# A decoder trunk on one core: two pieces of VectorE's work given to GpSimd

## The reference

```python
def s5_block(h, ...):
    xr = jnp.einsum('bsgc,gpc->bsgp', u, bbr)          # 64 groups, 64 states
    xi = jnp.einsum('bsgc,gpc->bsgp', u, bbi)
    _, _, sr, si = lax.associative_scan(combine, (a_r, a_i, xr, xi), axis=1)   # complex, along tokens
    ...
def peer(h, wq, subkeys, u_tab, v_tab):
    sv, si = lax.top_k(sc, PEER_TOPK)                  # 16 best keys of each half
    cand = sv[:, :, 0, :, None] + sv[:, :, 1, None, :]
    cidx = si[:, :, 0, :, None] * PEER_NKEYS + si[:, :, 1, None, :]
    cs, cpos = lax.top_k(cand.reshape(t, PEER_HEADS, -1), PEER_TOPK)
    idx = jnp.take_along_axis(cidx.reshape(t, PEER_HEADS, -1), cpos, axis=-1)
    gate = jax.nn.softmax(cs, axis=-1)
    act = jax.nn.gelu(jnp.einsum('td,tkd->tk', xbb, u_tab[ib]))
    return jnp.einsum('tk,tkd->td', gb * act, v_tab[ib])
```

## Time and profile before

| | |
|---|---|
| median of three runs | 1553.53 us (1551.04 to 1553.55) |
| the profiled execution | 1553.37 us, its span 1551.6 us |
| TensorE busy | 1097.8 us (71%) |
| VectorE busy | 1111.5 us (72%) |
| ScalarE busy | 770.2 us (50%) |
| GpSimd busy | 589.4 us (38%) |
| DMA | 603.39 MB, mean 389 GB/s |

### The profile page before, as it was taken

The page is one execution under the profiler, slowest core; times in us unless marked ns, Lnnn a source line. Parts: engine busy times, 40 slices in busy tenths (PEclk is TensorE's granted clock), DMA queues, the critical chain, the costliest instruction groups (busy, mean ns, idle before and its releaser), DMA issues.

```text
span 1551.6 us, 19133 instructions
## 1 busy us (share of the span) xinstructions
PE 1097.8 (71%) x5920; PEld 348.4 (22%) x5920; DVE 1111.5 (72%) x2533; ACT 770.2 (50%) x2120; POOL 589.4 (38%) x517
## 2 busy tenths in 40 slices
PE   7997678866765666679866575656878666666665
PEld 3542222322211212223221121212323111111110
DVE  2356887479787899985477799999456866666554
ACT  2315554445456667764334666766334644444433
POOL 0024343323443354554334345344432443434430
PEclk9998689878966776879988567686998777676675
DMA  9569999999999998999999999999999999999995
GB/s 358 179 234 413 420 405 418 414 415 408 415 421 421 354 374 358 410 421 415 412 413 414 403 357 369 355 363 406 380 416 415 415 422 421 421 421 421 421 422 234
DMA packets 105418, 603.39 MB, mean 389 GB/s; under 512 B 9314, under 2 KB 9442, under 8 KB 39780
## 3 DMA queue, kind: packets, MB, share of 16 engines
q0 software_dynamic: 73728, 536.90, 84.8%
q1 hardware_dynamic: 31588, 65.26, 11.3%
HBM read 601.08 MB, written 1.05 MB: 388 GB/s over the span
## 4 chain that ended last, share of the span: by engine, by line
DMA 32%; DVE 31%; PE 22%; ACT 7%; issue 3%; DVEq 3%; ACTq 1%; POOL 1%; SPq 0%; POOLq 0%
DMA rings<-in_uv_tab_dram,idx 24%; DVE rings L1324 11%; PE ps L715 9%; PE ps L920 8%; DMA wst<-in_wq_dram 7%; DVE mem L1231 2%; PE ps L908 2%; DVE dgs L1324 2%; ACT dgs L667 1%; DVE mem L1213 1%; ACT wgt L664 1%; DMA rings<-in_w_in_dram 1%; DVE mem L1242 1%; ACT L661 1%; DVE mem L1240 1%
## 5 line engine op out<-in xcount | busy, mean ns | idle before, releaser
L920 PE MATMUL ps<-rings,dgs 64*64 64x512 f32 x3648 | 638.0, 804 | 343.3 <-ACT dgs L667 342.6
L463 POOL DMA_INDIRECT rings<-in_uv_tab_dram,idx x456 | 521.7, 1144 | 804.3 <-PE ps L920 687.8
L1324 DVE CUSTOM_DVE_ANT_0 rings<-rings,h 128x1024 f32<-128x1024 f32 x456 | 550.7, 1224 | 210.8 <-DMA rings<-in_uv_tab_dram,idx 197.7
L661 ACT ACTIVATE gel<-dots 128x1 f32<-128x1 f32 x512 | 102.1, 199 | 522.2 <-DVE dots L1324 518.5
L920 PEld LDWEIGHTS ps<-rings,dgs 64*64 64x64 f32 x3648 | 128.3, 163 | 783.4 <-ACT dgs L667 682.3
L667 ACT ACTIVATE dgs<-cst,wgt 128x128 f32<-128x128 f32 x512 | 205.6, 402 | 36.3 <-issue 1.5
L715 PE MATMUL ps<-wst,hT 128*128 128x512 f32 x320 | 168.0, 666 | 37.1 <-DMA wst<-in_wq_dram 20.5
L664 ACT ACTIVATE wgt<-gel,share 128x1 f32<-128x1 f32 x512 | 150.8, 295 | 35.5 <-issue 0.3
L920 PE MATMUL ps<-dgs 64*64 64x512 f32 x448 | 80.2, 795 | 53.2 <-ACT dgs L667 53.1
L463 POOL DMA_INDIRECT dgs<-in_uv_tab_dram,idx x56 | 65.9, 1176 | 88.3 <-PE ps L920 74.8
L715 PEld LDWEIGHTS ps<-wst,hT 128*128 128x128 f32 x320 | 63.4, 212 | 138.1 <-issue 134.9
(11 more groups left out here) (192 smaller groups left out, 991.2 us busy)
## 6 DMA issues: line engine op xcount, KB each, us to landing
wst<-in_wq_dram SPq DMA_DIRECT2D x15, 2048.0 KB, 28.2
wst<-in_w_out_dram SPq DMA_DIRECT2D x4, 2048.0 KB, 22.8
wst<-in_glu_w_dram SPq DMA_DIRECT2D x4, 2048.0 KB, 31.7
rings<-in_uv_tab_dram,idx POOLq DMA_INDIRECT x456, 15.7
rings<-in_w_in_dram SPq DMA_DIRECT2D x3, 2048.0 KB, 16.7
rings<-in_w_in_dram SPq DMA_DIRECT2D x2, 1024.0 KB, 7.5
dgs<-in_w_in_dram SPq DMA_DIRECT2D x1, 2048.0 KB, 19.4
vec<-in_vecs_dram SPq DMA_DIRECT2D x3, 512.0 KB, 17.2
```

The costliest lines, as they stand in the source:

```text
L463: nc.gpsimd.indirect_dma_start(out=ring[g % RING], out_offset=None, in_=uv_tab, in_offset=bass.IndirectOffsetOnAxis(ap=idx[n % AHEAD][:, s ...
L661: A.activation(gel[i][:, every], dots[i][:, every], ACT.Gelu_apprx_tanh)
L920: ins = PE.matmul(ps[64 * b:64 * b + 64, 4 + 2 * t + half, :], diag[rows, g % DIAGS, rows], ring[g % RING][rows, D + b * BANK:D + (b + 1) ...
L1324: V.tensor_tensor_reduce(out=u, in0=u, in1=h[:, t, :], scale=1.0, scalar=0.0, op0=ALU.mult, op1=ALU.add, accum_out=dots[n % 2][:, s:s + 1] ...
```

## The change

Two pieces of VectorE's work move to GpSimd.

- `s5_add`: the two sums run on GpSimd, which waits for w_ok and raises a new semaphore add_ok. `s5_scan` on VectorE waits for add_ok; the small addition of the last tile's state (t = 1) stays on VectorE, now in `s5_scan`. The scan moves from slot + 3 to slot + 5 and `s5_back` from slot + 5 to slot + 6; `s5_out` stays at slot + 6.
- `route_index`: splitting and comparing (L1298 to L1301) become the end of `route_best` (slot + 4), which then raises pos_ok. The product and the sum over 16 run on GpSimd, the sum as a tree of four additions, then the addition of the two halves and a copy, with a drain after each. `hot` has a buffer of its own, `hot_p`. The factor 128 of the first half is put into the key numbers already. `route_best` of the next group waits for idx_ok before it writes them. Group 0 keeps its path on VectorE (`route_first`).

GpSimd runs its stages POOL_LAG = 6 rows later in its own loop: those of row g - 6 stand before the gather of row g. The nine gathers' depth lets GpSimd be ahead of the other engines by about that much.

```diff
@@ -35,6 +35,7 @@
 EXPERTS = NK * NK
 GROUPS = 2 * T * PH
 RING = 9
+POOL_LAG = 6
 AHEAD = 16
 PACE = 1
 DIAGS = 16
@@ -75,7 +76,7 @@
 ROUTE_AT = {1: 0, 2: 16, 3: 26, 4: 40, 5: 50, 6: 72, 7: 80, 8: 88, 9: 96, 10: 104, 11: 112, 12: 120, 13: 134, 14: 150,
             15: 166, 16: 234, 17: 242, 18: 250, 19: 260, 20: 276, 21: 292, 22: 308, 23: 324, 24: 362, 25: 370, 26: 378,
             27: 400, 28: 416, 29: 432, 30: 448, 31: 464}
-ROUTE_ALL = [(name, 0) for name, _ in ROUTE]
+ROUTE_ALL = [("route_first" if name == "route_index" else name, 0) for name, _ in ROUTE]
 
 
 PRELUDE = [("norm_T", 0), ("hT_copy", 0), ("norm_sq", 0), ("norm_ms", 0), ("norm_sd", 0), ("norm_r", 0),
@@ -168,9 +169,9 @@
             at(g, slot, ("s5_decay", t, c))
             at(g, slot + 1, ("s5_rot", t, c))
             at(g, slot + 2, ("s5_add", t, c))
-            at(g, slot + 3, ("s5_scan", t, c))
+            at(g, slot + 5, ("s5_scan", t, c))
             at(g, slot + 4, ("s5_cmat", t, c))
-            at(g, slot + 5, ("s5_back", t, c))
+            at(g, slot + 6, ("s5_back", t, c))
             if c + 1 < KC:
                 at(g, slot + 3, ("s5_turns", t, c + 1))
                 at(g, slot + 4, ("s5_frac", t, c + 1))
@@ -286,6 +287,7 @@
         pos_i = sb("pos_i", [P, TOPK], U32)
         pos_ab = sb("pos_ab", [P, 2, TOPK], U32)
         row = sb("row", [P, 2, TOPK])
+        hot_p = sb("hot_p", [P, 512])
         idx = [sb(f"idx{i}", [P, TOPK], U32) for i in range(AHEAD)]
         cs, gexp, dots, gel, wgt = (
             [sb(f"{n}{i}", [P, TOPK]) for i in range(2)] for n in ("cs", "gexp", "dots", "gel", "wgt"))
...
@@ -452,8 +456,39 @@
             nc.gpsimd.affine_select(out=sg3, in_=sg3, pattern=[[0, 8], [1, P]], compare_op=ALU.is_ge, fill=0.0, base=0,
                                     channel_multiplier=-1).then_inc(sgm_ok, 1)
 
+            def s5_add(t, c):
+
+                pool.wait_ge(w_ok, KC * t + c + 1)
+                nc.gpsimd.tensor_tensor(by_cos[:, 0, :, :], by_cos[:, 0, :, :], by_sin[:, 1, :, :], ALU.add)
+                nc.gpsimd.tensor_tensor(by_cos[:, 1, :, :], by_cos[:, 1, :, :], by_sin[:, 0, :, :],
+                                        ALU.subtract).then_inc(add_ok, 1)
+
+            hot = hot_p[:, :].rearrange("p (a k) -> p a k", k=TOPK)
+            hot2 = hot_p[:, :].rearrange("p (i a k) -> p i a k", i=2, k=TOPK)
+
+            def route_index(n):
+
+                pool.wait_ge(pos_ok, n)
+                nc.gpsimd.tensor_tensor(hot2, hot2, top_f[:, :, :].unsqueeze(2).to_broadcast([P, 2, TOPK, TOPK]), ALU.mult)
+                pool.drain()
+                for w in (8, 4, 2, 1):
+                    nc.gpsimd.tensor_tensor(hot[:, :, 0:w], hot[:, :, 0:w], hot[:, :, w:2 * w], ALU.add)
+                    pool.drain()
+                nc.gpsimd.tensor_tensor(hot2[:, 0, :, 0], hot2[:, 0, :, 0], hot2[:, 1, :, 0], ALU.add)
+                pool.drain()
+                nc.gpsimd.tensor_copy(idx[n % AHEAD][:, :], hot2[:, 0, :, 0]).then_inc(idx_ok, 1)
+
+            stage = dict(s5_add=s5_add, route_index=route_index)
+
+            def run(stages):
+                for name, *args in stages:
+                    if name in stage:
+                        stage[name](*args)
+
             for g in range(GROUPS * TOPK):
                 n, s = g // TOPK, g % TOPK
+                if g >= POOL_LAG:
+                    run(WORK[(g - POOL_LAG) // TOPK].get((g - POOL_LAG) % TOPK, []))
                 if s == 0:
                     pool.wait_ge(idx_ok, n + 1)
                 if g < RING and g % 2 == 0:
@@ -1214,17 +1249,13 @@
                 V.tensor_tensor(by_sin, x4, sin, ALU.mult).then_inc(w_ok, 1)
                 dve.drain()
 
-            def s5_add(t, c):
-                V.tensor_tensor(by_cos[:, 0, :, :], by_cos[:, 0, :, :], by_sin[:, 1, :, :], ALU.add)
-                V.tensor_tensor(by_cos[:, 1, :, :], by_cos[:, 1, :, :], by_sin[:, 0, :, :], ALU.subtract)
-                dve.drain()
+            def s5_scan(t, c):
+
+                dve.wait_ge(add_ok, KC * t + c + 1)
                 if t == 1:
 
                     V.tensor_tensor(by_cos[:, :, :, 0], by_cos[:, :, :, 0], z_last[:, :, 4 * c:4 * c + 4], ALU.add)
                     dve.drain()
-
-            def s5_scan(t, c):
-
                 dve.wait_ge(dt5_ok, KC * t + c + 1)
                 for r in range(2):
                     w = by_cos[:, r, :, :].rearrange("p j s -> p (j s)")
...
@@ -1281,7 +1312,9 @@
 
                 top_cs = cs[n % 2]
                 V.max(top_cs[:, 0:8], cand_a)
-                V.tensor_scalar(top_f[:, 0, :], top_i[:, 0, :], float(NK * (n // (T * PH))), None, ALU.add)
+                if n:
+                    dve.wait_ge(idx_ok, n)
+                V.tensor_scalar(top_f[:, 0, :], top_i[:, 0, :], float(NK * (n // (T * PH))), float(NK), ALU.add, ALU.mult)
                 V.tensor_copy(top_f[:, 1, :], top_i[:, 1, :])
                 dve.drain()
                 V.max_index(pos_i[:, 0:8], top_cs[:, 0:8], cand_a)
@@ -1292,20 +1325,22 @@
                 dve.drain()
                 V.max_index(pos_i[:, 8:16], top_cs[:, 8:16], cand_b).then_inc(cs_ok, 1)
                 dve.drain()
-
-            def route_index(n):
-
                 V.tensor_scalar(pos_ab[:, 0, :], pos_i[:, :], 4, None, ALU.logical_shift_right)
                 V.tensor_scalar(pos_ab[:, 1, :], pos_i[:, :], 15, None, ALU.bitwise_and)
                 dve.drain()
-                V.tensor_tensor(hot, bc(pos_ab[:, :, :].rearrange("p i a -> p (i a)"), [None, TOPK]),
-                                bc(iota16, [2 * TOPK, None]), ALU.is_equal)
-                dve.drain()
+                ins = V.tensor_tensor(hot, bc(pos_ab[:, :, :].rearrange("p i a -> p (i a)"), [None, TOPK]),
+                                      bc(iota16, [2 * TOPK, None]), ALU.is_equal)
+                if n:
+                    ins.then_inc(pos_ok, 1)
+                dve.drain()
+
+            def route_first(n):
+
                 V.tensor_tensor(hot2, hot2, top_f[:, :, :].unsqueeze(2).to_broadcast([P, 2, TOPK, TOPK]), ALU.mult)
                 dve.drain()
                 V.tensor_reduce(row[:, :, :].rearrange("p i a -> p (i a)"), hot, AX.X, ALU.add)
                 dve.drain()
-                V.scalar_tensor_tensor(idx[n % AHEAD][:, :], row[:, 0, :], float(NK), row[:, 1, :], ALU.mult,
+                V.scalar_tensor_tensor(idx[n % AHEAD][:, :], row[:, 0, :], 1.0, row[:, 1, :], ALU.mult,
                                        ALU.add).then_inc(idx_ok, 1)
 
             def route_gate(n):
...
```

More of the change, by code:

```diff
@@ L322, in trunk @@
         r_ok, rd_ok, sn_done, dt5_ok, dd_ok = (sem(n) for n in ("r_ok", "rd_ok", "sn_done", "dt5_ok", "dd_ok"))
+        add_ok = sem("add_ok")
+        pos_ok = sem("pos_ok")
         sq_done, ms_done, sd_done, h_done, nT_done, hT_act, hT_dve, x_done, w_used = (sem(n) for n in (
@@ L1251, in glu_sum @@
                 V.scalar_tensor_tensor(xs, gate[:, cols_], 0.5, xs, ALU.mult, ALU.add).then_inc(x_done, 1)
-            hot = cand[:, :].rearrange("p (a k) -> p a k", k=TOPK)
-            hot2 = cand[:, :].rearrange("p (i a k) -> p i a k", i=2, k=TOPK)
+            hot = hot_p[:, :].rearrange("p (a k) -> p a k", k=TOPK)
+            hot2 = hot_p[:, :].rearrange("p (i a k) -> p i a k", i=2, k=TOPK)
             def route_keys(n):
@@ L1330, in _ @@
                          s5_b0=s5_b0, s5_b1=s5_b1, s5_rot=s5_rot,
-                         s5_frac=s5_frac, s5_add=s5_add, s5_scan=s5_scan, s5_back=s5_back, glu_sum=glu_sum, norm_r=norm_r)
-            stage |= dict(route_keys=route_keys, route_pairs=route_pairs, route_best=route_best, route_index=route_index,
+                         s5_frac=s5_frac, s5_scan=s5_scan, s5_back=s5_back, glu_sum=glu_sum, norm_r=norm_r)
+            stage |= dict(route_keys=route_keys, route_pairs=route_pairs, route_best=route_best, route_first=route_first,
                           route_gate=route_gate)
```

## The result

The changed kernel takes 1771.5 us (median of four, 1766.5 to 1772.7) against 1553.5: a ratio of 1.140, 95% interval 1.137 to 1.143. That is 218 us more. The sign was forecast, but the size lies far above the range of 1532 to 1592 us. The profiled execution took 1766.5 us, its span 1764.7.

What follows compares the result with a forecast made beforehand. VectorE was taken to bound two S5 stretches, the DMAs most of the rest. 1553.4 + 7.7 (net VectorE loss) + 7 (late gathers) gave 1568 us, own range 1558 to 1580, range for all 1532 to 1592.

Steps and rivals of the forecast that it cites:

- The bound: VectorE limits two S5 stretches of some 300 us, DMAs nearly everything else; at most 39 us can be won.
- Cost in the full-DMA stretches: Outside the S5 stretches, 15.7 us from gather issue to landing covers delays of 4 to 11 us; routes cost nothing.
- The scan two rows later: Waiting on add_ok in S5 costs nothing, as four dots (4.6 us) lie between; up to 1 us a chunk if late.
- The later `s5_back`: One row later, TensorE waits some 2 us longer at s5_out, covered by filled ring slots.
- The price of a sum: A GpSimd sum of 512 elements takes 1.05 us (0.48 to 1.59), a route's seven operations 2.6 us.
- Holding: GpSimd's SBUF reads and VectorE's two-SBUF-input operations exclude each other: net loss 0.65 us per chunk, 0.85 per route.
- Rival A: At the dots behind the turn VectorE isn't held; 32 us return less some 6: 1528 us, chance 0.26.
- The sum without the omitted steps: Whole kernel: 1553.4 us before, plus 7.7 net VectorE loss in S5, plus 7 for delayed gathers: 1568 us.
- late gathers: GpSimd issues gathers later in the S5 stretches, half a microsecond per chunk or route: 7 us, bounds 0 and 15.
- Rival B: GpSimd sets the pace in the S5 stretches at 1.59 us a sum, VectorE idles: 1590 us, chance 0.15.

Runs made afterwards that it cites:

- places alone: Kernel before, nothing on GpSimd: six routes moved off or closer around the S5 rows, scan and s5_frac at slot + 5, s5_back at slot + 6; 1531.7 us.
- spare sum: Kernel before plus 48 unused GpSimd sums of 128x512, one in front of every third gather of the S5 rows; 1581.1 us, ratio 1.0172.

## Why the prediction was wrong, point by point

- **The bound.** Right for the kernel before, as far as was tried. Two stretches are bound by VectorE and most of the rest by the DMAs, and places alone won 22 us, of the 39 that were named as the most to be won.
- **Cost in the full-DMA stretches: "routes there cost nothing".** This is the step that failed. It counted the waits and the sums ahead of the next gather (4 to 11 us, against 15.7 us from issue to landing) and left the drains out of the count. They stood in the diff "with a drain after each" and got no price at all. A drain doesn't delay the issue by a given time that a filled queue covers; it ends when the queue is empty, so no depth of queue covers it. Each stood 7 to 25 us and went with some 7 us in which no gather moved. Drains: some 190 of 218 us (1771.5 to 1581.8 when they alone are replaced).
- **The scan two rows later: "so nothing".** Wrong. Only add_ok was examined, not what the scan's old place had hidden on VectorE: 18 us alone, from `s5_frac` waiting for ScalarE.
- **The later `s5_back`.** Right: 34.1 us of waits on TensorE (16 of 2.1 us) remain with the loss gone.
- **The price of a sum.** GpSimd's sum of 512 lasts 1.26 us where nothing holds it (1.05 only where both inputs are the same piece), not 1.05, and a route's seven operations 3.4 us, not 2.6. The Trainium skill (GPSIMD Engine Reference, "Elementwise — side-by-side cycle accounting") gives 4497 ns for a sum of 2048 elements. A quarter of that, an estimate of 1.12 us, is nearer than the price used, and the trace's 1.26 is higher still.
- **Holding.** Right in kind: dots of 2.27 us, and reads cost 28 us where writes cost 3. In size a spare sum held VectorE for 0.7 us on average and cost 0.6 us of the span. The row with 0.12 us of holding doesn't bear out the prediction's "as long as that GpSimd read could last": `affine_select` ran 0.26 us beyond VectorE's start there. Rival A is refuted, and GpSimd's work is no relief while it holds VectorE: 12 us lost by the route part without drains, and 3 to 10 by the sums.
- **The sum without the omitted steps.** 1568 us was forecast, and the whole change with the drains replaced and `s5_frac` moved takes 1573. The forecast was about right for a kernel that it wasn't made for. That is partly luck: how these 19 us divide between holding (7.7 in the sum) and late gathers (7) wasn't measured, and some of the loss lies in rows where the sum had none.
- **Rival B, GpSimd sets the pace.** Its 1590 us lay nearest, but for another reason. Its sign did appear, with VectorE 84 and 82% busy in the S5 stretches (100.75 of 120.5 and 183.67 of 225.0 us) and waiting for gathers. But by busy time GpSimd is at 42%; what set the pace was its standing still, also in the tail, where the rival had no cost.

## What to carry to other kernels

In a list of moved operations, price the synchronisation too, on the engine where it now stands: a drain that costs VectorE some 0.07 us costs the engine that issues the gathers a whole refill of the DMA queue (here some 3.4 us of the time with nothing behind it, about 7 with a chain of small sums behind it). Have such an engine wait for its own semaphore instead. And before a stage changes its row, look at what ran beside it: the cover that it gave to a neighbour's wait can be worth more than the work that is moved.

## What was not expected of the hardware

- GpSimd's drain ended about 1.2 us behind the last landing of gathers in flight (DMA share 0.00 from 1459.0 us, the next sum at 1460.25), and without gathers in flight further drains between sums took some 0.1 us. Whether it waits for the landing itself or for its own bookkeeping of the descriptors isn't told apart by these runs. It doesn't wait for SyncE's transfers: where the sum behind a drain starts at 229.58 us, the last packet of a gather ends at 228.5, and from 228.6 to 229.6 us the changed kernel's queues show only q1, which is SyncE's, at full use:

```profile
q1 hardware_dynamic: 129, 0.39, 100.2%
```

- VectorE's TENSOR_SCALAR on 128x16 was held too, with one tensor from SBUF: 1.04 us at 574.68 above (its factor is one value for each partition), where the group's mean was 0.23 before. Those with only constants beside the tensor were held as well: `top_f<-top_i` has a mean of 0.23 us with the spare sums, 0.16 before. The Trainium skill (SBUF — State Buffer, "Who interferes with whom") says that `tensor_scalar` can enter a mode that takes both ports; these runs show the holding and not the mode. The prediction had counted only operations with two SBUF inputs.
- Of the 35 us that the spare sums held VectorE, about four fifths became time. What became of the rest isn't shown.
